# Sparse attention's scores: fp32r products over a split, stacked query in place of fp32 products

## The reference, cut to what matters

```python
s_c = einsum('bgrqd,bgnd->bgrqn', qb, kc) - slopes * dist_c     # 31 compressed keys
o_c = masked_softmax(s_c, end_c <= t) @ vc
s_s = einsum('bgrqd,bgqkd->bgrqk', qb, ks) - slopes * dist_s    # selected keys, causal
o_s = masked_softmax(s_s, pos_s <= t) @ vs
s_w = einsum('bgrqd,bgkd->bgrqk', qb, kw) - slopes * dist_w     # window keys, causal
o_w = masked_softmax(s_w, mask_w) @ vw
o = gate0 * o_c + gate1 * o_s + gate2 * o_w
```

## Time and profile before

| what | us |
|---|---|
| median of 3 runs (lowest, highest) | 1510.56 (1506.25, 1511.45) |
| profiled execution, its own time | 1508.93 |
| its span | 1507.1 |
| GLA stage, from the trace | about 165 to 262 |
| NSA stage, from the trace | about 262 to 437 |
| granted clock of TensorE, mean | 0.995 |

### The profile page before, as it was taken

One profiled execution on the slowest core, in us unless ns is written; L12 is line 12 of the kernel. 1 busy time (PEld: TensorE's weight loads), 2 busy tenths in 40 slices (PEclk: granted clock), 3 DMA queues, 4 the chain that ended last, 5 costly groups with the idle time before them and its releaser, 6 DMA issues.

```text
span 1507.1 us, 20189 instructions
## 1 busy us (share of the span) xinstructions
PE 1493.6 (99%) x7328; PEld 1180.8 (78%) x7328; DVE 659.6 (44%) x1092; ACT 581.1 (39%) x909; POOL 653.7 (43%) x304
## 2 busy tenths in 40 slices
PE   9999999999999999999999999999999999999999
PEld 6888788666678877888888886877768888888887
DVE  6221444765552458333331015888756433343000
ACT  5131332655463335222333224566654322232211
POOL 4434312663224433444444543666224444444443
PEclk9999999999999999999999999999999999999999
DMA  5522211111112223222323332421113322222333
GB/s 195 167 71 84 84 42 42 43 56 44 53 61 98 89 80 98 95 94 93 96 95 103 107 109 87 147 77 57 56 57 98 97 95 91 96 94 97 112 100 124
DMA packets 38542, 135.05 MB, mean 90 GB/s; under 512 B 4544, under 2 KB 4800, under 8 KB 38224
## 3 DMA queue, kind: packets, MB, share of 16 engines
q1 hardware_dynamic: 37296, 130.70, 26.6%
q10 hardware_dynamic: 1184, 3.51, 0.7%
HBM read 132.09 MB, written 2.10 MB: 89 GB/s over the span
## 4 chain that ended last, share of the span: by engine, by line
PE 74%; issue 15%; DVE 5%; POOL 4%; ACT 1%; DMA 0%; POOLq 0%; SPq 0%; DVEq 0%; ACTq 0%
PE bank L1065 18%; PE bank L1066 18%; PE bank L1067 18%; POOL wL L426 3%; PE bank L1399 2%; PE bank L1400 2%; PE bank L1401 2%; PE bank L1094 2%; PE bank L1096 2%; PE bank L1095 2%; DVE bank L2057 1%; PE bank L1454 1%; PE bank L1261 1%; PE bank L1297 1%; PE bank L1256 1%
## 5 line engine op out<-in xcount | busy, mean ns | idle before, releaser
L426 POOL TENSOR_TENSOR wL<-raw,wH 128x1024 fp32r<-128x1024 f32 x234 | 572.5, 2447 | 799.8 <-ACT wH L522 636.1
L522 ACT ACTIVATE wH<-raw 128x1024 fp32r<-128x1024 f32 x209 | 221.2, 1059 | 605.9 <-PE bank L1067 562.6
L1065 PE MATMUL bank<-aH,wH 128*128 128x512 f32 x984 | 385.5, 392 | 1.1 <-POOL wL L426 0.9
L1067 PE MATMUL bank<-aH,wL 128*128 128x512 f32 x984 | 383.6, 390 | 0.0
L1066 PE MATMUL bank<-aL,wH 128*128 128x512 f32 x984 | 383.6, 390 | 0.0
L1065 PEld LDWEIGHTS bank<-aH,wH 128*128 128x128 f32 x984 | 185.1, 188 | 44.2 <-issue 2.5
L1066 PEld LDWEIGHTS bank<-aL,wH 128*128 128x128 f32 x984 | 185.1, 188 | 38.7 <-issue 0.5
L1067 PEld LDWEIGHTS bank<-aH,wL 128*128 128x128 f32 x984 | 185.0, 188 | 38.5
L1066 PE MATMUL bank<-fL,wH 128*128 128x512 f32 x352 | 137.0, 389 | 0.0
L1065 PE MATMUL bank<-fH,wH 128*128 128x512 f32 x352 | 137.0, 389 | 0.0
L1067 PE MATMUL bank<-fH,wL 128*128 128x512 f32 x352 | 136.9, 389 | 0.0
(11 more groups left out here) (306 smaller groups left out, 1904.0 us busy)
## 6 DMA issues: line engine op xcount, KB each, us to landing
raw<-in_w SPq DMA_DIRECT2D x234, 512.0 KB, 3.3
bmk<-in_bias SPq DMA_DIRECT2D x6, 512.0 KB, 4.7
xT<-in_x SPq DMA_DIRECT2D x8, 256.0 KB, 5.8
out_x<-xT SPq DMA_DIRECT2D x8, 256.0 KB, 3.8
ct<-in_ct ACTq DMA_DIRECT2D x3, 384.0 KB, 3.4
w1k<-in_w1k ACTq DMA_DIRECT2D x1, 1024.0 KB, 5.8
w1v<-in_w1v ACTq DMA_DIRECT2D x1, 1024.0 KB, 5.0
raw<-in_w SPq DMA_DIRECT2D x2, 256.0 KB, 3.8
```

Of the source, the lines that this page charges most:

```text
L426: pool.tensor_tensor(wL[:, c_slot, :], raw[:, c_slot, :], wH[:, c_slot, :].bitcast(F32), ALU.subtract).then_inc(sem("w_lo"), 1)
L522: act.activation(wH[:, s, :], raw[:, s, :], ACT.Copy).then_inc(sem("w_hi"), 1)
L1065: pe.matmul(bank[:], hi, H[:, ka, :], start=(k == 0), stop=False)
L1067: mm = pe.matmul(bank[:], lo, H[:, ka, :], start=False, stop=(k == p.k - 1))
```

## The change

The nine steps a pair stay. What is different:

- Scores are fp32r products. `qst` has a slot for each group in which the high part of the group's query stands in the group's own 64 partitions and the low part in the other 64. The keys of each group stand twice, in both halves of the partitions, once as high parts and once as low parts (`KX`, eight tiles; they lie over slots of `pj` that are free by then, and one over `nt_`). A score is then two products of 128 rows (`part` 0 and 1).
- For that ACT makes the high parts of the keys in `in1` (`high_of_keys`, 4 instructions of 64x512 a branch), DVE the low parts (`low_of_keys`, 4 a branch); DVE makes both for the compressed keys (`kcx`, 8 instructions of 64x32) at the head of NSA; ACT makes the high parts of the queries (2 instructions instead of 1 a pair, one step earlier) and DVE the low parts (`low_of_queries`, 2 of 64x512 a pair).
- `scores(0)` now waits for all of these.
- `silu` of tile n moves from step n + 2 to step n + 1, the step of its `tanh`.
- `root_of_heads` is eight instructions of 128x512 in buffers outside `pj`, instead of two of 128x2048.
- The input x is loaded as tiles 0, 1 and three pairs instead of eight tiles. Two sets of semaphores of the feed-forward parts become one.

```diff
             def scores(s, r, j):
                 if j == 0:
-                    pe.wait_ge(sem("nsa_q"), r + 1)
+                    pe.wait_ge(sem("nsa_qlo"), (r + 1) * NG)
+                if s == 0:
+                    pe.wait_ge(sem("keys_c"), 8)
+                    pe.wait_ge(sem("keys_lo"), 8)
...
                 if j == 0:
-                    for i in range(TT):
-                        for g in range(NG):
-                            mm = pe.matmul(B[SBANK[g]][:, i * NCP:(i + 1) * NCP], qst[rows[g], r % 2, i * P:(i + 1) * P],
-                                           kcT[rows[g], :], start=True, stop=True)
+                    for g in range(NG):
+                        for i in range(TT):
+                            for part in range(2):
+                                mm = pe.matmul(B[SBANK[g]][:, i * NCP:(i + 1) * NCP], qst[:, r % 2, g, i * P:(i + 1) * P],
+                                               kcx[:, g, part, :], start=(part == 0), stop=(part == 1))
...
                 for g in range(NG):
-                    pe.matmul(B[SBANK[g]][:, 0:(i + 1) * P], qst[rows[g], r % 2, i * P:(i + 1) * P],
-                              kT[br][rows[g], 0:(i + 1) * P], start=True, stop=True).then_inc(sem("nsa_s"), 1)
+                    for br, i, cols in windows(j):
+                        for part in range(2):
+                            mm = pe.matmul(B[SBANK[g]][:, cols], qst[:, r % 2, g, i * P:(i + 1) * P],
+                                           KX[br, g, part][:, 0:(i + 1) * P], start=(part == 0), stop=(part == 1))
+                    mm.then_inc(sem("nsa_s"), 1)
```

```diff
-        TANH_AT = {(0, j + 1): j for j in range(KD)}
-        SILU_AT = {(0, j + 2): j for j in range(KD - 1)} | {(1, 1): KD - 1}
+        TANH_AT = {n + 1: (n,) for n in range(KD)}
+        SILU_AT = {n + 1: tiles for n, tiles in TANH_AT.items()}
```

On ACT:

```diff
+            def high_of_keys(br):
+                for g, rows in enumerate(group_rows):
+                    for half in (rows, group_rows[1 - g]):
+                        act.activation(KX[br, g, 0][half], KSRC[br][rows], ACT.Copy).then_inc(sem("keys_hi"), 1)
...
-            group(p, 16)
+            group(p, 16, 2)
+            act.wait_ge(sem("kin_ready"), 4)
+            act.wait_ge(sem("v_S"), 2)
+            high_of_keys(0)
+            group(p, 18, 2)
...
-            group(p, 24, 3)
+            group(p, 24, 1)
+            high_of_keys(1)
+            group(p, 25, 2)
...
             def queries(r):
-                act.activation(qst[:, r % 2, :], pj[:, NQ + r, :], ACT.Copy, scale=DH ** -0.5 * 2.0 ** r).then_inc(sem("nsa_q"), 1)
+                for g, rows in enumerate(group_rows):
+                    act.activation(qst[rows, r % 2, g, :], pj[rows, NQ + r, :], ACT.Copy, scale=DH ** -0.5 * 2.0 ** r)\
+                        .then_inc(sem("nsa_qhi"), 1)
...
-                act.activation(rs4, bT[:], ACT.Ln).then_inc(sem("gla_rs"), 1)
-                act.wait_ge(sem("gla_rs"), 1)
-                act.activation(rs4, rs4, ACT.Exp, scale=-0.5).then_inc(sem("gla_rs"), 1)
+                for h in range(GH):
+                    act.activation(rs4[h], bT[:, h, :], ACT.Ln).then_inc(sem("gla_rs"), 1)
+                for h in range(GH):
+                    act.wait_ge(sem("gla_rs"), h + 1)
+                    act.activation(rs4[h], rs4[h], ACT.Exp, scale=-0.5).then_inc(sem("gla_rs"), 1)
...
-                if j == 4 and r < NR - 1:
+                if j == 3 and r < NR - 1:
                     queries(r + 1)
```

On DVE:

```diff
+            def low_of_keys(br):
+                for g in (1, 0):
+                    rows, other = group_rows[g], group_rows[1 - g]
+                    dve.wait_ge(sem("keys_hi"), 4 * br + 4)
+                    if g == 0:
+                        dve.wait_ge(sem("keys_lo"), 4 * br + 2)
+                    for half in (other, rows):
+                        dve.tensor_tensor(KX[br, g, 1][half], KSRC[br][rows], KX[br, g, 0][rows].bitcast(F32), ALU.subtract)\
+                            .then_inc(sem("keys_lo"), 1)
+                        if g == 0 and half is other:
+                            dve.wait_ge(sem("keys_lo"), 4 * br + 3)
+            low_of_keys(0)
...
             group(6, 3)
+            low_of_keys(1)
...
             dve.wait_ge(sem("gla_head"), GH + 1)
+            dve.wait_ge(sem("cmp_out"), 1)
+            for g, rows in enumerate(group_rows):
+                for n, half in enumerate((rows, group_rows[1 - g])):
+                    dve.tensor_copy(kcx[half, g, 0, :], kcT[rows, :]).then_inc(sem("keys_c"), 1)
+                dve.wait_ge(sem("keys_c"), 4 * g + 2)
+                for half in (rows, group_rows[1 - g]):
+                    dve.tensor_tensor(kcx[half, g, 1, :], kcT[rows, :], kcx[rows, g, 0, :].bitcast(F32), ALU.subtract).then_inc(sem("keys_c"), 1)
+            def low_of_queries(r):
+                for g, rows in enumerate(group_rows):
+                    dve.wait_ge(sem("nsa_qhi"), r * NG + g + 1)
+                    dve.scalar_tensor_tensor(qst[group_rows[1 - g], r % 2, g, :], pj[rows, NQ + r, :], DH ** -0.5 * 2.0 ** r,
+                                             qst[rows, r % 2, g, :].bitcast(F32), ALU.mult, ALU.subtract).then_inc(sem("nsa_qlo"), 1)
+            low_of_queries(0)
...
-                if (r, j) in SILU_AT:
-                    n = SILU_AT[r, j]
+                if j == 4 and r < NR - 1:
+                    low_of_queries(r + 1)
+                for n in SILU_AT.get(s, ()):
                     dve.wait_ge(sem("r_tanh"), n + 1)
```

More of the change, by code:

```diff
@@ L215, in two_blocks_kernel @@
         nr = sb("nr", [P, S])
+        with ExitStack() as over:
+            keys_too = sb("keys_too", [P, S], F32R, over)
         nt_ = sb("nt_", [P, S])
@@ L220, in two_blocks_kernel @@
         sc1 = ExitStack()
+        with ExitStack() as over:
+            sb("under_keys", [P, MISC, S], F32, over)
+            keys = sb("keys", [P, KWT + 1 - MISC, S], F32R, over)
         pj = sb("pj", [P, 35, S], F32, sc1)
@@ L229, in two_blocks_kernel @@
         w2v = sb("w2v", [P, DH], F32, sc1)
[L230 removed]
+        spare = sb("spare", [P, S], F32, sc1)
+        wa2 = spare[0:RANK, :]
         with ExitStack() as early:
@@ L324, in two_blocks_kernel, with windows, key_blocks, heads_before @@
         maskc = cst("maskc").rearrange("p (i g n) -> p i g n", g=NG, n=NCP)
-        TANH_AT = {(0, j + 1): j for j in range(KD)}
-        SILU_AT = {(0, j + 2): j for j in range(KD - 1)} | {(1, 1): KD - 1}
-        NSTEPS = [(r, j) for r in range(NR) for j in range(1 + 2 * TT)]
-        PER_R = 1 + 2 * TT
-        def branch_tile(j):
-            return (j - 1) // TT, (j - 1) % TT
+        TANH_AT = {n + 1: (n,) for n in range(KD)}
+        SILU_AT = {n + 1: tiles for n, tiles in TANH_AT.items()}
+        WINDOWS = ((),) + tuple(((br, i),) for br in range(2) for i in range(TT))
+        PER_R = len(WINDOWS)
+        NSTEPS = [(r, j) for r in range(NR) for j in range(PER_R)]
+        HEADS_OF_R = NG * sum(len(w) for w in WINDOWS)
+        def windows(j):
+            at, out = 0, []
+            for br, i in WINDOWS[j]:
+                out.append((br, i, slice(at, at + (i + 1) * P)))
+                at += (i + 1) * P
+            return out
+        def key_blocks(j):
+            return [(br, i, kt) for br, i in WINDOWS[j] for kt in range(i + 1)]
+        def heads_before(r, j):
+            return r * HEADS_OF_R + NG * sum(len(w) for w in WINDOWS[:j])
+        def maxima_before(r, j):
+            return heads_before(r, j) + NG * (r + (j > 0))
+        def gates_of(r, j):
+            (br, i), last = WINDOWS[j][0], WINDOWS[j][-1]
+            if len(WINDOWS[j]) == 1:
+                return gview_of(r)[:, 1 + br, i:i + 1, :]
+            return gview_of(r)[:, 1 + br, i:last[1] + 1:last[1] - i, :] if last[0] == br else gview_of(r)[:, 1 + br:2 + last[0], i, :]
+        def gview_of(r):
+            return gates[:].rearrange("p i (g r b) -> p r b i g", g=NG, r=NR)[:, r]
         def upd_bank(c):
@@ L355, in two_blocks_kernel, with over_slot @@
         SBANK, TBANK, OBANK = (2, 3), (0, 4), (5, 6)
-        P_OF_R = 2 * TT * NG
+        def over_slot(n):
+            return keys[:, n - MISC, :]
+        KX = {(0, 0, 0): over_slot(KCT), (0, 1, 0): over_slot(VCT), (0, 1, 1): over_slot(VST), (0, 0, 1): over_slot(KST),
+              (1, 0, 0): over_slot(VWT), (1, 1, 0): keys_too[:], (1, 1, 1): over_slot(MISC), (1, 0, 1): over_slot(KWT)}
+        KSRC = (pj[:, KST, :], pj[:, KWT, :])
+        group_rows = [slice(g * DH, (g + 1) * DH) for g in range(NG)]
+        P_OF_R = (PER_R - 1) * NG
         T_OF_R = P_OF_R + 1
@@ L750, in heads_out @@
                 act.activation(pj[:, NQ + r, :], B[OBANK[r % 2]][:], ACT.Copy).then_inc(sem("nsa_out"), 1)
-            for r, j in NSTEPS:
+            for s, (r, j) in enumerate(NSTEPS):
                 if j == 0:
@@ L1310, in turned @@
                     return
-                k = r * 2 * TT + j - 1
```

(20 more changed lines are left out.)

136 lines of the change are left out of this document (68 added, 68 removed).

## The result

The changed kernel takes 1516.9 us (median of seven runs, 1514.6 to 1519.36) beside 1507.06 for the kernel before in the same comparison: a ratio of 1.0061, 95% interval 1.0049 to 1.0073, which is 9.2 us (the two medians lie 9.8 apart). It is slower, as forecast, and inside the range, but by a third less than the 13.1 us of the sum, and partly for other reasons. The forecast of 1523 was counted from a median of 1510.56 of three runs of the kernel before; with seven runs that median is 1507.06, so 3.5 of the 6.1 us between 1523 and 1516.9 are the base, and the sum is compared with the 9.2 in what follows.

The account below looks back on a forecast made before the run. PE bounds the kernel, busy 99% of the span. Terms 4.7 + 6.5 + 2.5 = 13.7, less 3 x 0.2, gave 13.1 on the median 1510.56: 1523.7, stated as 1523 us; range 1513 to 1531.

Parts of the forecast that it names:

- head of GLA: Between the last eviction and GLA's first work: low_of_keys(1), interrupted by POOL's low part, delays PE's transposes by 2.5 us.
- head of NSA, to scores(0) and its step: scores(0) waits for DVE's splits, PE starts 4.0 late, its step 0.7 longer: 4.7 us, bounds 3.5 and 5.6.
- first pair, steps 3 to 11: First head pair of NSA: DVE's silu waits for its tanh, delaying masked_max and scores; 6.5 us, from 1.6 to 9.
- later pairs, to step 35: Second head pair of NSA onward: score products 0.2 us a pair cheaper, over three pairs, with no silu delay.
- Both signs: Would show the forecast wrong: pairs 2 to 4 shorter by over 1 us each, or silus that never wait.
- these 0.2: Head of NSA: the four compressed-key copies, if they also wait for POOL, add 0.2 us; left out of the sum.
- up to 1.3 in step 4: First head pair: the second pair's low queries on DVE add up to 1.3 us before step 4's silu.
- rival (b): Not slower: narrow products under the floor, pairs 2 to 4, gain 2.1 or 3.1 each; 1508 or 1515; chance 0.08.
- (a): Half the delays hidden: GLA's head 0, NSA's head 3.5, silu loop 3.5; +7 us, 1517; chance 0.22.
- (c): Narrow products at the fp32 rate, silu loop at 9, or both, later low queries too: 1525 to 1530; chance 0.2.
- (d): Score products carried out as fp32 over the whole array: some 12 us a pair, 1560; chance 0.02.
- At no cost: high_of_keys and low_of_keys(0) in idle time of ACT and DVE, feed-forward semaphores: nothing; x pairs: 0.5 either way.

Follow-up runs that it names:

- e3: Changed kernel with low_of_keys(1) two evictions earlier, between the evictions of tiles 24 and 25 of in1: 1514.63 us, ratio 1.0043.
- e10: Changed kernel with five fp32 products of no use in PE's queue ahead of scores(0), all else the same: 1513.56 us, ratio 1.0039.
- e12: e8 plus the compressed keys split during in1 and the next pair's low queries behind masked_max in step 6: 1504.38 us, ratio 0.9979.
- e1: Changed kernel with the last silu back in step (1, 1), as in the kernel before: 1515.62 us, ratio 1.0051.
- e8: Changed kernel with units of gate products before scores(0), root_of_heads first, last silu one step later, low_of_keys(1) earlier, queries' high and low parts later: 1506.35 us, ratio 0.9993.
- e5: Changed kernel with part 0 of the scores alone, the products against the keys' low parts left out: 1511.71 us in its one run.
- e11: e5 with each score product over its group's own 64 rows, so the queries' low parts are left out too: 1512.23 us in its one run.
- e2: Changed kernel with x loaded as eight single tiles, as before: 1516.39 us, ratio 1.0058.
- e4: Changed kernel with six units of gate_products moved ahead of scores(0), taken from later steps of the first pair: 1515.4 us, ratio 1.0051.
- e6: Kernel before with all eight silus one step earlier, in the step of their tanh: 1518.06 us, ratio 1.0074.

## Why the prediction was right and where it wasn't

| term | forecast | measured |
|---|---|---|
| head of GLA | +2.5 | +2.4 |
| head of NSA, to scores(0) and its step | +4.7 | +8.5 to step 3 |
| first pair, steps 3 to 11 | +6.5 | +2.8 |
| later pairs, to step 35 | -0.6 | -4.9 |
| drain behind step 35 | 0 | +0.5 |
| sum | 13.1 | 9.3 |

That the time fell into the range is partly luck. The largest term, 6.5 of the 13.1, stood for an edit that the change doesn't make; what came in its place are a slow clock and smaller delays on the one side and a gain in the later pairs on the other, none of which the sum had in this size. Both signs that the prediction named for being wrong came: the later pairs are shorter by over 1 us each, and the silus don't wait.

**Head of GLA: right,** in size, place and releaser. POOL's low part came between DVE's four instructions as forecast, and e3 took the wait away alone.

**Head of NSA: right place, too small.** Scores(0) did wait, for DVE's low_of_queries, and started 4.8 later. Without its longer step the forecast was 4.0. The terms given there (264.2, 0.7, twice 0.6 and 0.1) add up to 266.2 and not to its 266.4, so the terms give 3.8 and the start is 1.0 later than they have it. The bill for small instructions failed: they were costed at 0.1 and cost 0.2 each, the upper bound that the text gave. DVE's own rows at the head of NSA in after:

```profile
264.15 1.27 DVE L1920 CAST kcx<-kcT 64x32 fp32r<-64x32 f32 x2
265.46 0.40 DVE L1923 TENSOR_TENSOR kcx<-kcT,kcx 64x32 fp32r<-64x32 f32 x2
265.89 0.38 DVE L1920 CAST kcx<-kcT 64x32 fp32r<-64x32 f32 x2
266.31 0.41 DVE L1923 TENSOR_TENSOR kcx<-kcT,kcx 64x32 fp32r<-64x32 f32 x2
266.75 1.40 DVE L1929 SCALAR_TENSOR_TENSOR qst<-pj,qst 64x512 fp32r<-64x512 f32 x2
```

The first two copies took 1.27 us and the next two, of the same shape, 0.38. POOL's low part ran from 262.84 to 265.19. So the copies too are held while POOL runs, by which they end at 265.42, 0.2 behind POOL. The Trainium skill (SBUF — State Buffer, section Who interferes with whom) names copies and casts among the operations that can take the ports shared with GpSimd, and the trace agrees; the prediction had set these 0.2 aside in a sentence. The six small ones behind them take 1.3 where the sum had 0.7, and the two low parts of the queries 1.4 where it had 1.2. The three make the 1.0.

What the sum had no term for is the 3.7 us between step 0 and step 3. The longer step of compressed keys is 0.7 of it, as forecast (at step 18, with the full clock, 1.78 from its start to the next dense product against 1.01 before). 2.3 is the clock (e10). In windows of one microsecond at the start of NSA:

```profile
267.00:268.00 1.00, 0.00 (x0) 0.00 (x0) 0.97 (x2) 0.00 (x0) 0.00 (x0) 0.50 0.86 344
...
272.00:273.00 1.00, 1.00 (x3) 0.80 (x3) 0.93 (x3) 0.00 (x0) 0.00 (x0) 0.50 0.00 0
276.00:277.00 1.00, 1.00 (x5) 0.73 (x4) 0.00 (x0) 1.00 (x3) 0.81 (x1) 0.74 0.00 0
277.00:278.00 1.00, 1.00 (x6) 0.76 (x5) 0.00 (x0) 0.98 (x3) 0.92 (x2) 1.00 0.00 0
```

PE stood still for 4.87 us until 268.25. Its granted clock falls to 0.50, the 1.2 GHz level, within the wait, and is back at 1.00 only at 277, when PE had worked for over 8 us. The compressed step, 16 products, takes 3.57 us there and 1.85 in e12 at full clock. The text had read the clock (1.00 in both stages) and drawn nothing from it. The step that failed is to have costed a wait of 4 us on PE at 4 us. The remaining 0.7 was not taken apart; e10 itself has the clock at 0.50 for three of these microseconds, so it may be the clock as well.

**First pair: wrong step, a range that held.** The forecast of 6.5 (1.6 to 9) rests on silus that the change doesn't move. The 2.8 comes from elsewhere. 1.7 is the one silu that moves (e1): at the end of step (1, 0) it stands ahead of masked_max of step (1, 1) on DVE, and PE waits 1.4 for that. The other 1.1 lies in steps 4 to 6, where step 5 to step 6 takes 6.1 us against 4.5 before. There the queries' high part on ACT delays the exponentials, and low_of_queries(1) on DVE the maximum. In after, ACT, then DVE, then the waits on PE:

```profile
291.65 1.27 ACT L775 ACTIVATE qst<-pj 64x512 fp32r<-64x512 f32 x2
...
295.84 1.40 DVE L1929 SCALAR_TENSOR_TENSOR qst<-pj,qst 64x512 fp32r<-64x512 f32 x2
...
296.71 1.18 PE L1386 MATMUL bank<-ct,pS 128*128 128x128 f32 x8 [0.74 <-ACT pS L812]
...
298.44 0.50 PE L1366 MATMUL bank<-keys,qst 128*128 128x256 f32 x2 [0.56 <-DVE nmx L1972]
```

The prediction had the DVE half of it ("up to 1.3 in step 4") and not ACT's. That these two account for the 1.1 is read from the waits, and in e8 and e12, which move both, step 5 to step 6 takes 4.4 and 4.3. They move the silu and the head's work with them, so the 1.1 hasn't been isolated.

**Later pairs: the sign right, the size too small by far,** 4.9 for 0.6. The products themselves cost what was forecast: 0.23, 0.18, 0.12 and 0.11 from one start to the next for 512, 384, 256 and 128 columns (after's four products less e5's two, halved), and 1.78 for the 16 of 32 columns, 0.11 each. So the floor of 0.11 was the right value and rival (b)'s columns-only price was wrong; that it is the weight load that makes the floor stays an inference from its 0.11. What the sum missed is a price that the old products paid and the new ones don't. The same step of the third pair in before and in after:

```profile
365.76 0.66 PE L1316 MATMUL bank<-ct,pS 128*128 128x128 f32 x4
366.35 1.13 PE L1297 MATMUL bank<-pj,qst 64*128 64x512 f32 x4
367.41 0.50 PE L1094 MATMUL bank<-aH,wH 128*128 128x512 f32 x1
367.75 0.39 PE L1095 MATMUL bank<-aL,wH 128*128 128x512 f32 x1
```

```profile
376.48 0.66 PE L1386 MATMUL bank<-ct,pS 128*128 128x128 f32 x4
376.89 1.17 PE L1366 MATMUL bank<-keys,qst 128*128 128x512 f32 x4
377.90 0.39 PE L1160 MATMUL bank<-aH,wH 128*128 128x512 f32 x1
378.13 0.39 PE L1161 MATMUL bank<-aL,wH 128*128 128x512 f32 x1
```

The scores take 1.06 and 1.01, as costed. But they start 0.59 behind the transposes before and 0.41 after: 0.18 a step (it is 0.17 to 0.18 in nearly all) over the 24 steps from 11 to 35 is 4.3, and with the products' own 0.2 a pair it is 4.8 of the measured 4.9. The 0.11 behind the next dense product (0.34 against 0.23) is the one that the sum did count. e11 against e5 shows that the rows of the product are the cause and not fp32: with 64 rows of fp32r the 0.17 and the 0.11 are back. The Trainium skill (TensorEngine Tiling (Array Packing), section Key Properties) states that a change of the tiling mode drains TensorE. The 0.17 fits that; that a drain is what takes it, no run shows. The prediction read the price of a step from one score step to the dense stream behind it and never from the instruction ahead of it. That is the step that failed: both edges of an instruction whose shape changes have a price.

**Rivals.** (a) came closest, +7 for the measured 9.2, by other means: the delays at the two heads weren't hidden, that of the silus was never there, and the later pairs paid back a part. (b) was right about place and direction and wrong about its cause; the 24 steps gave 4.9, where it had 9.3 in three pairs, and 1.8 a pair is less than the 2.3 from which it decides with (a)'s delays. (c) and (d) didn't happen.

**At no cost** holds for the x pairs (e2). For high_of_keys and low_of_keys(0) no wait of PE in `in1` stands against it; neither was tested alone.

## What to carry to other kernels

A wait on a full engine can cost more than its length: look whether its clock drops behind it, and put work that is due anyway ahead of the waiting instruction, checking which engine is late next (e4 exchanged one wait for another). A change of an instruction's format is priced at both of its edges, from the rows ahead of and behind it. And before a schedule's entry is costed, evaluate the expression that builds it: here the largest term of the sum was a key read one too low.

## What was not expected of the hardware

- A TensorE wait of 4.9 us cost another 2.3 behind it, the clock being granted at 0.50 until PE had worked for some 8 us. Products without use in the wait gave these 2.3 back, though the clock still fell for three microseconds (e10). Behind shorter waits (0.92 and 1.41) the same fall came in some runs and not in others, for some 1.5 us.
- A product over 64 rows starts 0.17 to 0.18 later behind a 128-row one than one over 128 rows does, and the first dense product behind it is followed after 0.34 instead of 0.23 (e11, e5).
- Eight silus one step earlier cost 9.7 us (e6), though each is 0.68 long where nothing holds it up.
- Copies of 64x32 from fp32 to fp32r on DVE were held by POOL as instructions with two sources are: two took 1.27, and 0.38 with POOL idle.
